# Attention maxima and sums in one table of 68 columns, turned by four transposes instead of twelve

## What is computed

```python
m = jnp.max(scores, axis=-1, keepdims=True)
p = jnp.exp(scores - m)
l = jnp.sum(p, axis=-1, keepdims=True)
out = jnp.einsum('bdhnqk,bdhnke->bdhnqe', p, vw.astype(jnp.float32)) / l
lse = (m + jnp.log(l))[..., 0]
...
o = jnp.stack(outs, axis=2)
lse = jnp.stack(lses, axis=2)
alpha = jax.nn.softmax(lse, axis=2)
o = (o * alpha[..., None]).reshape(B, S, ATTN_WIDTH).astype(u.dtype)
return o @ w_out
```

## Time and profile before

| | |
|---|---|
| median of 3 runs | 2097.58 us (2096.8 to 2097.99) |
| span of the profiled execution | 2095.4 us |
| TensorE busy, products | 2087.4 us, 11210 products |
| TensorE weight loads | 1739.3 us |
| VectorE, ScalarE, GpSimd busy | 1035.4, 736.8, 1141.8 us |
| moved by DMA | 204.40 MB, mean 98 GB/s |

### The profile page before, as it was taken

The page is one execution under the profiler, slowest core; times in us unless marked ns, Lnnn a source line. Parts: engine busy times, 40 slices in busy tenths (PEclk is TensorE's granted clock), DMA queues, the critical chain, the costliest instruction groups (busy, mean ns, idle before and its releaser), DMA issues.

```text
span 2095.4 us, 28286 instructions
## 1 busy us (share of the span) xinstructions
PE 2087.4 (100%) x11210; PEld 1739.3 (83%) x11210; DVE 1035.4 (49%) x1217; ACT 736.8 (35%) x859; POOL 1141.8 (54%) x822
## 2 busy tenths in 40 slices
PE   9999999999999999999999999999999999999998
PEld 8888888888888889888888888888888888888887
DVE  6487654555113356634555333744477544553226
ACT  6336532212224455443122233515433332222244
POOL 6677555555455433365555555544566555555553
PEclk9999999999999999999999999999999999999999
DMA  5222132222332222242222222222222222223321
GB/s 199 82 67 78 50 112 100 100 87 94 105 115 105 86 80 82 81 141 100 90 91 100 100 102 101 100 99 101 99 88 94 101 100 100 94 88 109 119 101 62
DMA packets 33210, 204.40 MB, mean 98 GB/s; under 512 B 3688, under 2 KB 6504, under 8 KB 9456
## 3 DMA queue, kind: packets, MB, share of 16 engines
q1 hardware_dynamic: 32896, 203.13, 27.8%
q10 hardware_dynamic: 240, 0.23, 0.0%
HBM read 200.19 MB, written 2.10 MB: 97 GB/s over the span
## 4 chain that ended last, share of the span: by engine, by line
PE 98%; DVE 0%; DMA 0%; ACT 0%; SPq 0%; issue 0%; DVEq 0%; ACTq 0%
PE bank L2086 98%; DMA first_raw<-wall 0%; DVE x L1960 0%; PE bank L2474 0%; PE bank L2365 0%; PE bank L2501 0%; SPq L624 0%; ACT w_hi L822 0%; DVE h L2062 0%; PE bank L2476 0%; ACT un L822 0%; PE bank L2226 0%; ACT rr L822 0%; DVE ao_lo L1892 0%; ACT first_whi L822 0%
## 5 line engine op out<-in xcount | busy, mean ns | idle before, releaser
L682 POOL TENSOR_TENSOR w_lo<-raw,w_hi 128x512 fp32r<-128x512 f32 x676 | 977.1, 1475 | 859.0 <-ACT w_hi L822 859.0
L2086 PE MATMUL bank<-u_hi,w_hi 128*128 128x512 f32 (+1 forms) x1936 | 753.2, 389 | 0.1
L2086 PE MATMUL bank<-u_lo,w_hi 128*128 128x512 f32 (+1 forms) x1936 | 749.7, 388 | 0.0
L822 ACT ACTIVATE w_hi<-raw 128x2048 fp32r<-128x2048 f32 x185 | 354.2, 1915 | 924.8 <-PE bank L2086 921.7
L2086 PE MATMUL bank<-u_hi,w_lo 128*128 128x512 f32 (+1 forms) x1936 | 482.2, 388 | 0.0
L2086 PEld LDWEIGHTS bank<-u_hi,w_hi 128*128 128x128 f32 x1936 | 363.6, 188 | 74.7 <-ACTq L1236 0.5
L2086 PEld LDWEIGHTS bank<-u_lo,w_hi 128*128 128x128 f32 x1936 | 363.9, 188 | 73.4
L2086 PEld LDWEIGHTS bank<-u_hi,w_lo 128*128 128x128 f32 x1936 | 362.6, 188 | 74.4
L2086 PE MATMUL bank<-act_hi,w_hi 128*128 128x512 f32 x528 | 205.6, 389 | 0.0
L2086 PE MATMUL bank<-act_lo,w_hi 128*128 128x512 f32 x528 | 205.5, 389 | 0.0
L1375 DVE TENSOR_TENSOR h<-h,bank 128x512 f32<-128x512 f32 x48 | 30.8, 684 | 300.7 <-PE bank L2086 300.7
(11 more groups left out here) (302 smaller groups left out, 2124.1 us busy)
## 6 DMA issues: line engine op xcount, KB each, us to landing
raw<-wall SPq DMA_DIRECT2D x185, 1024.0 KB, 4.9
out_t<-h SPq DMA_DIRECT2D x8, 256.0 KB, 2.3
h<-x_t SPq DMA_DIRECT2D x3, 512.0 KB, 7.8
first_raw<-wall SPq DMA_DIRECT2D x6, 256.0 KB, 7.7
av_moved<-av SPq DMA_DIRECT2D x14, 64.0 KB, 2.1
h<-x_t SPq DMA_DIRECT2D x2, 256.0 KB, 3.4
first_raw<-wall SPq DMA_DIRECT2D x4, 128.0 KB, 3.7
lmask_f<-lmask_in SPq DMA_DIRECT2D x1, 512.0 KB
```

Of the source, the lines that this page charges most:

```text
L682: ins = nc.gpsimd.tensor_tensor(w_lo[:, s, c], raw[:, s, c], w_hi[:, s, c].bitcast(F32), ALU.subtract)
L822: return nc.scalar.activation(out, in_, func, **k)
L2086: return nc.tensor.matmul(out, lhsT, rhs, start=start, stop=stop, skip_group_check=True)
```

## The change

The tables get 68 columns per block, `ROWS = 2 * CUT + GH` with CUT = 32 and GH = 4. Head hd stands in column `32 * (hd // 4) + hd % 4`, so that the three groups come out of one transpose in partitions 0 to 3, 32 to 35 and 64 to 67 of one bank. The columns between hold what was in the memory before, and their rows are not read. One table then takes four transposes, one per block of queries, all into bank 5. The tables of their own are gone: `mst` now lies in `ssq2` and `lst` in `rstd2`, buffers not in use then. Everything allocated behind the old tables moves down by 384 bytes per partition.

```diff
+ROWS = 2 * CUT + GH
+
+
+def row_of(hd):
+    return CUT * (hd // GH) + hd % GH
...
-        mst = sb("mst", [P, AH, TT])
-        lst = sb("lst", [P, AH, TT])
...
+        mst, lst = (t[:, 0:ROWS * TT].rearrange("p (g n) -> p g n", n=TT) for t in (ssq2, rstd2))
...
-            t = PB[5 + g][0:GH, :]
+            t = PB[5][CUT * g:CUT * g + GH, :]
             return by_residue(t, g) if g else in_order(t)
...
-                             accum_out=lst[:, hd, n:n + 1])
+                             accum_out=lst[:, row_of(hd), n:n + 1])
...
-                ch.step(nc.vector.tensor_reduce(mst[:, hd, :], s_h, AX_X, ALU.max))
+                ch.step(nc.vector.tensor_reduce(mst[:, row_of(hd), :], s_h, AX_X, ALU.max))
...
-                for g in range(3):
-                    for n in range(TT):
-                        ins = nc.tensor.transpose(PB[5 + g][0:GH, n * P:(n + 1) * P],
-                                                  src[:, GH * g:GH * (g + 1), n], ident[:])
+                for n in range(TT):
+                    ins = nc.tensor.transpose(near(PB[5][0:ROWS, :], n), src[:, :, n], ident[:])
                 ins.then_inc(done, 1)
```

More of the change, by code:

```diff
@@ L1778, in maxima @@
                 ch.settle()
-                ch.step(nc.vector.tensor_reduce(mst[:, hd, :], s_h, AX_X, ALU.max))
+                ch.step(nc.vector.tensor_reduce(mst[:, row_of(hd), :], s_h, AX_X, ALU.max))
                 if hd < GH:
                     ch.link(nc.vector.tensor_reduce(cols[:, r + 3, 1:TT], s_ab[1][:, 1:TT, :], AX_X, ALU.max))
-                    ch.step(tt(mst[:, hd, 1:TT], mst[:, hd, 1:TT], cols[:, r + 3, 1:TT], ALU.max))
+                    ch.step(tt(mst[:, row_of(hd), 1:TT], mst[:, row_of(hd), 1:TT], cols[:, r + 3, 1:TT], ALU.max))
                 ch.settle()
-                ts(cols[:, r + 1, :], mst[:, hd, :], -ATT_SCALE, None, ALU.mult).then_inc(max_ready, 1)
+                ts(cols[:, r + 1, :], mst[:, row_of(hd), :], -ATT_SCALE, None, ALU.mult).then_inc(max_ready, 1)
             def head_sums(hd):
@@ L1789, in head_sums @@
                 if hd < GH:
-                    ch.step(tt(lst[:, hd, 1:TT], lst[:, hd, 1:TT], cols[:, r + 3, 1:TT], ALU.add))
+                    ch.step(tt(lst[:, row_of(hd), 1:TT], lst[:, row_of(hd), 1:TT], cols[:, r + 3, 1:TT], ALU.add))
             def attended(hd):
```

## The result

| | before | changed |
|---|---|---|
| median of 5 runs | 2097.58 us (2096.8 to 2098.29) | 2146.41 us (2145.25 to 2147.96) |
| ratio, 95% interval | | 1.0234 (1.0223 to 1.0245) |
| span of the profiled execution | 2095.4 us | 2144.3 us |

The prediction was 2095.8 us, with a range of 2094.6 to 2097.7. The measured time is 48.8 us above the kernel before, and nothing in the change's own instructions is that large.

What follows compares the result with a forecast made beforehand. PE's own stream was taken to bound the kernel. Two transpose blocks saving 0.87 us each, 1.75 us in all, took the median from 2097.58 to 2095.83 us, other terms costing nothing; range 2094.6 to 2097.7.

Steps and rivals of the forecast that it cites:

- What bounds the kernel: Whole span: TensorE busy 2087.4 of 2095.4 us, so a microsecond cut from PE's stream is one of the span.
- What is removed: Two transpose blocks at 836 and 843 us: each 0.44 us in place of 1.31, saving 1.75 us for both.
- The seam: First products after a block start 0.44 us apart where 0.235 is usual; this 0.2 us was left in place.
- The strided load of 68 columns: Transposes' operand load, columns 16 bytes apart: estimated some 178 ns, mostly overlapped, leaving a period of 0.109 us.
- The near end of the bounds: Period of the 68-column transposes: 0.109 us each, against a far end of 0.235 us that saves only 0.74 us.
- Rival C: Transpose blocks: strided loads do not hide, load and product add up, 0.73 us slower, 2098.3 us; chance 0.04.
- Who is late next: Engines feeding PE after the blocks: second block's margin falls from 1.4 to about 0.5 us, still no wait.
- rival A: Second block: PE waits for sums_ready, losing at most the first block's 0.87 us, 2096.7 us; chance 0.07.
- The margin ahead of the first factor product: DVE's idle ahead of L1798 falls from 1.51 to 0.36 us, so PE still sets that point.
- What is moved: Instruction order unchanged; six DVE reads from partitions 32 and 64 of bank 5 cost nothing more, at most +0.36 us each.
- Rival B: Gain given back at a later wait, or by the 384-byte shift of everything behind the tables: 2097.6 us; chance 0.06.
- The chance of "slower": Whole kernel: probability 0.02 that the change is slower by over 0.2%.

Runs made afterwards that it cites:

- e1: The changed kernel with 384 bytes per partition put back ahead of u, so u and act stand where they did before: 2096.06 us, ratio to before 0.9993.

## Why the prediction was wrong, point by point

**What bounds the kernel.** Right, and it carried the error: PE's stream is the time. I asked who waits for whom and never asked what a product's 0.2257 us depend on. No row that I had read could say: the main products of the kernel before all stood at a multiple of 256 bytes, and at that distance they keep their 0.2257 us.

**What is removed.** Right to 0.01 us: 0.44 for 1.31, twice. The seam stayed, and the changed trace shows the two products after the block 0.44 us apart (852.51 and 852.95).

**The strided load of 68 columns.** Estimated 178 ns, measured 140 to 143: the term was 36 ns too long, on the safe side. The near end of the bounds was right: the period is 0.109 us. Rival C fell. Of the two rules of the Trainium skill that spoke for it, the one on 16-byte lines is not refuted: 68 columns at a stride load as long as 128 adjacent ones (142 and 140 ns), but the load's length does not reach the period. The one on row groups I read too narrowly. The same section of "TensorE: Matmul & The Clock Gate" of the Trainium skill (Part 3, "The mechanism") also lets a load go ahead of running products when it fills the background weight buffer. In this trace loads of 142 ns at a period of 110 ns overlap; which buffer they fill no run shows.

**Who is late next.** No wait at the second block: rival A did not happen. The margin ahead of the first factor product was mis-sized. I left DVE 0.36 us of idle; it had none, because L1871's three products took 4.74 us and not 2.96 once POOL's work came earlier (in e1, at the good distance). I moved PE and DVE ahead and left POOL where it was, though its low half is released by PE. This cost 0.3 us at the first factor product.

**What is moved.** Not quite nothing. Each read of the bank lasts about 10 ns longer (678 to 686 ns at L1853's heir, 668 to 679 before). The three of L1853 together took 1.87 us before and 2.07 after, since their starts lie further apart; the two of L1851 took 1.39 and 1.40. Whether the other partitions do it, or that all read one bank, was not tested. The 0.2 us at L1853 are hidden: DVE then waits 0.78 us for ACT. At L1865 they are not: in e1 DVE's chain is 0.62 us ahead of before at its first product, as forecast, and 0.39 us ahead at L1871.

**Rival B, where the answer was.** The step that failed is its price. I wrote that everything behind the tables moves by 384 bytes, called the shift a multiple of 128 to set it aside, and let it cost at most the 1.75 us of the gain, with 0.06 chance. No row that I had read shows a price per alignment, so it needed bounds on both sides, as the strided load had got: 6 ns on 8500 products is 50 us, and a shift that touches every product had to be bounded by a share of the whole stream, not by the size of the edit. The chance of "slower", 0.02, was wrong for the same reason: the mechanism was named, but it was only allowed to cancel.

## What to carry to other kernels

A change of the allocation can change the time of every product whose operands lie behind it: before costing the edit, list which tensors move, and keep the distance from the loaded to the streamed operand of the main products fixed, by a pad worked out from their addresses and not by a number. Here, with 512 streamed columns, the distance to keep was a multiple of 256 bytes. A small unused tensor between others may be holding such a distance; say so in the code. And an edit that makes the bound engine faster moves everything that it releases, so look for what the released work then runs beside.

## What the runs showed of the hardware

The time of a product of 128x128 by 128x512 depends on the distance in a partition between the loaded and the streamed operand: 14.65 us for 64 at a multiple of 256 bytes, 14.9 to 15.3 at nearly all others (14.75 at 252, once 14.77 at 64), with PE alone as in the kernel. "SBUF — State Buffer" of the Trainium skill calls PE's two read ports independent ("Who interferes with whom"); these runs show that their addresses matter to each other. What makes a distance slow was not tested, nor why 256 streamed columns turn the sign, nor another element type than this kernel's. Transposes with 4, 68 or 128 loaded columns all come every 0.11 us.
